# A two-layer decoder trunk on one core: r, k and v in three rounded products, sums by head in column groups, both low-rank rates together

## What is computed

```python
xx = x_prev - h
xr, xw, xk, xv, xa, xg = (h + xx * mu[j] for j in range(6))
r, k, v = xr @ w_r, xk @ w_k, xv @ w_v                       # 1024 x 1024 each
log_w = -softplus(-(dw0 + tanh(xw @ dw1) @ dw2)) - 0.5       # rank 64
a = sigmoid(aw0 + (xa @ aw1) @ aw2)                          # rank 64
g = sigmoid(xg @ gw1) @ gw2                                  # rank 128
kk = heads(k * k_k); kk = kk / max(sqrt(sum(kk * kk, -1)), 1e-12)
# state per head: S = S * w + (S @ -kk) kk*a + v k ;  y = S @ r   (scan over tokens)
y = groupnorm(y) * ln_w + ln_b + sum(r * k * r_k, -1) * v
out = (y * g) @ w_o
```

## Time and profile before

| | us |
|---|---|
| median of 3 runs | 3864.74 |
| lowest, highest | 3859.37, 3880.96 |
| the profiled execution | 3877.49 |
| its span, first to last instruction | 3875.8 |
| PE busy, matrix products | 3598.1 (93%) |
| DVE, ACT, POOL busy | 1759.1, 943.7, 525.5 |
| mean granted TensorE clock | 0.951 |

### The profile page before, as it was taken

One profiled execution on the slowest core, in us unless ns is written; L12 is line 12 of the kernel. 1 busy time (PEld: TensorE's weight loads), 2 busy tenths in 40 slices (PEclk: granted clock), 3 DMA queues, 4 the chain that ended last, 5 costly groups with the idle time before them and its releaser, 6 DMA issues.

```text
span 3875.8 us, 61931 instructions
## 1 busy us (share of the span) xinstructions
PE 3598.1 (93%) x23964; PEld 3078.7 (79%) x23964; DVE 1759.1 (45%) x3204; ACT 943.7 (24%) x1787; POOL 525.5 (14%) x220
## 2 busy tenths in 40 slices
PE   9999998998999999969999588989899899999997
PEld 6667666667999999946567477778785699999996
DVE  3545543116444444461240467655631544444444
ACT  2223324302111111111001455555520211111111
POOL 0000000001111122101000122223221121111120
PEclk9999999999999999989999789999869999999998
DMA  2222114402111111022111101000051111111101
GB/s 96 59 73 62 52 40 143 141 0 68 52 43 43 43 43 43 0 82 86 45 67 45 68 12 40 29 23 23 20 162 43 55 44 43 43 43 43 43 22 45
DMA packets 151310, 206.35 MB, mean 53 GB/s; under 512 B 42542, under 2 KB 126433, under 8 KB 150786
## 3 DMA queue, kind: packets, MB, share of 16 engines
q1 hardware_dynamic: 145122, 184.55, 14.4%
q0 software_dynamic: 6048, 19.73, 1.6%
HBM read 173.87 MB, written 50.82 MB: 58 GB/s over the span
## 4 chain that ended last, share of the span: by engine, by line
PE 64%; issue 7%; DVE 5%; PEld 4%; ACT 2%; DMA 1%; SPq 0%; POOL 0%; ACTq 0%; PEldq 0%; DVEq 0%; POOLq 0%
PE bank L429 61%; PEld bank L429 4%; PE bank L437 3%; DVE arena L2437 1%; DVE arena L2430 1%; ACT arena L2016 1%; DVE arena L2213 1%; DVE hT L2522 1%; DVE std L2210 0%; SPq L1260 0%; ACT arena L1943 0%; DVE n L2213 0%; DMA arena<-arena 0%; DVE arena L2456 0%; DVE arena L2504 0%
## 5 line engine op out<-in xcount | busy, mean ns | idle before, releaser
L429 PE MATMUL bank<-arena 128*128 128x384 f32 (+20 forms) x9432 | 1562.3, 351 | 142.2 <-ACT arena L1682 28.5
L429 PEld LDWEIGHTS bank<-arena 128*128 128x128 f32 (+11 forms) x9432 | 1124.7, 181 | 560.7 <-issue 171.2
L2225 DVE TENSOR_TENSOR hT<-hT,bank 128x384 f32<-128x384 f32 (+1 forms) x816 | 426.4, 526 | 523.5 <-PE bank L429 523.5
L429 PE MATMUL bank<-n_hi,up_hi 128*128 128x384 f32 (+1 forms) x1536 | 502.3, 327 | 27.2 <-DVE n_lo L2382 14.2
L1682 ACT COPY arena<-bank 128x512 f32<-128x512 f32 (+12 forms) x573 | 264.6, 497 | 1035.2 <-PE bank L429 755.4
L429 PE MATMUL bank<-u_hi,dn_hi 128*128 128x384 f32 (+1 forms) x1536 | 501.1, 326 | 0.0
L429 PE MATMUL bank<-u_lo,dn_hi 128*128 128x384 f32 (+1 forms) x1536 | 499.9, 325 | 0.0
L429 PE MATMUL bank<-n_hi,up_lo 128*128 128x384 f32 (+1 forms) x1536 | 499.6, 325 | 0.0
L429 PE MATMUL bank<-n_lo,up_hi 128*128 128x384 f32 (+1 forms) x1536 | 499.6, 325 | 0.0
L429 PE MATMUL bank<-u_hi,dn_lo 128*128 128x384 f32 (+1 forms) x1536 | 496.0, 323 | 0.0
L1521 POOL TENSOR_TENSOR up_lo<-arena,up_hi 128x2048 fp32r<-128x2048 f32 x32 | 151.2, 4725 | 1590.9 <-ACT up_hi L1838 1590.9
(11 more groups left out here) (181 smaller groups left out, 2903.5 us busy)
## 6 DMA issues: line engine op xcount, KB each, us to landing
arena<-in_ffn_w_up SPq DMA_DIRECT2D x32, 1024.0 KB, 5.4
arena<-in_ffn_w_down SPq DMA_DIRECT2D x32, 1024.0 KB, 7.4
arena<-past_scratch SPq DMA_DIRECT2D x32, 640.0 KB, 8.1
past_scratch<-in_cache_kv_latent SPq DMA_DIRECT2D x128, 128.0 KB, 2.4
hidden_scratch<-hT SPq DMA_DIRECT2D x1, 4288.0 KB, 13.8
past_scratch<-in_cache_k_rope SPq DMA_DIRECT2D x128, 32.0 KB, 2.1
arena<-in_rwkv_w_r SPq DMA_DIRECT2D x4, 1024.0 KB, 5.2
r_scratch<-arena POOLq DMA_DIRECT2D x8, 512.0 KB, 5.2
```

Source lines behind the costliest of these rows:

```text
L429: return pe.matmul(out, lhsT, rhs, start=first, stop=last, skip_group_check=group)
L2225: lane.do(dve.tensor_tensor(hT[:, k, at:at + w], hT[:, k, at:at + w], b[:, 0:w], ALU.add), ring.drained)
```

## The change

**Mixing stage.** r, k and v use three rounded products as the MLPs do. The differences are formed once (`DX`, by pieces), the mixed input `x_mix` exists for r, k and v only, by pieces; ACT rounds it to `x_hi`, DVE subtracts for `x_lo` (which lies where `x_mix` lay). ACT rounds each weight block to `w_hi`, POOL subtracts for `w_lo`. `x_hi` lies on `hT`, whose content is stored by then. The low-rank inputs are no longer mixed: since (h + xx·mu) @ w = h @ w + xx @ (mu·w), PE forms `nT` with the plain weights and adds `DX` with the weights times mu. dw1 and aw1 do this together, ahead of r; gw1 does it between r and k. All is written out, without loops.

```diff
+            def lora_sums(b, weights, acts, p, first, last):
+                at, w = PIECES[p]
+                for k in range(KT):
+                    ins = mm(b[:, 0:w], weights[:, k, :], acts[:, k, at:at + w], first and k == 0, last and k == KT - 1)
+                return ins
...
+            pe.wait_ge(wl_s, 32)
+            three = []
+            for p in range(3):
+                pe.wait_ge(norm_s, mark["normed1"] + p + 1)
+                three.append(ra.bank(ahead=p))
+                lora_sums(three[p], w_wa, nT, p, True, False)
+            pe.wait_ge(mu_s, 1)
+            for p in range(3):
+                pe.wait_ge(dx_s, p + 1)
+                ra.done(lora_sums(three[p], w_mu, DX, p, False, True))
+            pe.drain().then_inc(lora_used, 1)
```

```diff
             big(0, False)
-            lora_in(1, wl)
-            big(2, False)
-            lora_in(3, wl)
-            big(4, True)
-            lora_in(5, wg)
+            pe.wait_ge(wl_s, 48)
+            pe.wait_ge(mu_s, 2)
+            for p in range(3):
+                b = ra.bank()
+                lora_sums(b, w_g, nT, p, True, False)
+                ra.done(lora_sums(b, w_mu, DX, p, False, True))
+            big(1, False)
+            big(2, True)
```

```diff
+            for m in range(3):
+                mixed(m, 0)
+                mixed(m, 1)
+                split_mixed(m, 0)
+                mixed(m, 2)
+                split_mixed(m, 1)
+                split_mixed(m, 2)
+                if m == 0:
+                    dve.wait_ge(lora_used, 1)
+                    dve.wait_ge(wl_s, 48)
+                    dve.tensor_tensor(w_mu[:, :, :], w_g[:, :, :], prm[:, :, R_MU + 5:R_MU + 6].broadcast_to([P, KT, P]), ALU.mult).then_inc(mu_s, 1)
```

```diff
+            def big(m, token_major):
+                for blk in range(4):
+                    hi, lo = w_hi[blk % 2], w_lo[blk % 2]
+                    pe.wait_ge(wlo_s, 4 * m + blk + 1)
+                    for p, (at, w) in enumerate(PIECES):
+                        if blk == 0:
+                            pe.wait_ge(xlo_s, 3 * m + p + 1)
...
+                                    out = b[0:rows.stop - rows.start, u * 256:(u + 1) * 256]
                                     for k in range(KT):
-                                        ins = mm(b[0:w, u * 256:(u + 1) * 256], x[:, k, t * P:t * P + w], wb[par][:, k, :],
-                                                 k == 0, k == KT - 1)
+                                        mm(out, x_hi[:, k, rows], hi[:, k, :], k == 0, False)
+                                        mm(out, x_hi[:, k, rows], lo[:, k, :], False, False)
+                                        ins = mm(out, x_lo[:, k, rows], hi[:, k, :], False, k == KT - 1)
...
+                                cols = slice(m_ * P, (m_ + 1) * P)
+                                b = ra.bank()
+                                for k in range(KT):
+                                    mm(b[:, 0:w], hi[:, k, cols], x_hi[:, k, at:at + w], k == 0, False)
+                                    mm(b[:, 0:w], hi[:, k, cols], x_lo[:, k, at:at + w], False, False)
+                                    ins = mm(b[:, 0:w], lo[:, k, cols], x_hi[:, k, at:at + w], False, k == KT - 1)
+                                ra.done(ins)
+                        if blk == 3:
+                            through(xu_t)
+                    through(wbu_t)
+                    mark["blocks"].append(ra.filled.n)
```

```diff
+            split_weights(0)
+            for n in range(12):
+                if n + 1 < 12:
+                    split_weights(n + 1)
+                store_block(n)
```

```diff
+                pair = [ra.bank(ahead=1), ra.bank(free=True)][::-1]
+                ends = []
+                for k in range(4):
+                    for z in range(2):
+                        rows, ct = slice(z * RN, (z + 1) * RN), 4 * half + k
+                        ends.append(mm(pair[z][:, k * w:(k + 1) * w], w_lora[rows, ct * P:(ct + 1) * P], lc[rows, 0:w], True, True))
+                for ins in ends[-2:]:
+                    ra.done(ins)
...
+                for j in range(2):
+                    at = MIXTAB["head_cols"][0] + 2 - 2 * j
+                    for g in range(4):
+                        ins = mm(bank[32 * g:32 * g + 32, 0:w], mixtab[:, at:at + 32], kx[:, 4 * j + g, 0:w], j == 0, j == 1)
...
                 level_16(c, 0, ma, lambda: turn_b_k(c, P))
-                if prepare:
-                    decays(c + 1, wn, [0])
                 level_32(c, 0, ma, lambda: bonus_sums(c, P))
                 bonus_at = ra.filled.n - 1
                 v_in[par].wait(pe, nth)
                 level_64(0, ma, [when(prepare, lambda: key_sums(c + 1, wn)), lambda: first_sums(0), lambda: turn_bonus(P, bonus_at)])
-                finals(0, when(prepare, lambda: decays(c + 1, wn, [1])), when(prepare, lambda: key_scales(c + 1, wn)))
+                finals(0, when(prepare, lambda: rates(c + 1, wn, 0)), when(prepare, lambda: (rates(c + 1, wn, 1), key_scales(c + 1, wn))))
```

```diff
+                    for dst, row in ((sw, R_DW0), (rate, R_AW0)):
+                        b = ring.bank()
+                        for k in range(4):
+                            ct = 4 * half + k
+                            ins = act.activation(dst[:, ct, 0:w], b[:, k * w:(k + 1) * w], ACT.Sigmoid,
+                                                 bias=prm[:, ct, row:row + 1])
+                        lane.do(ins, ring.drained)
+                        if half == 1:
+                            signal(act.drain(), sw_b if dst is sw else rate_b)
...
                 spread_32(c, 0)
-                if prepare:
-                    decay_rates(c + 1, wn)
                 take_w_32()
...
-                    key_rates(c + 1, wn)
+                    both_rates(c + 1, wn)
                 spread_16(c, 1)
                 if prepare:
                     decays(c + 1, wn, wn == TAIL)
```

```diff
                 if finish:
                     centre(c - 1, P, Y[1 - par])
                 if prepare:
-                    sums(c + 1, wn, wn == TAIL)
...
                 new_half(0)
                 if prepare:
                     normed_keys(c + 1, wn)
+                    sums(c + 1, wn, wn == TAIL)
```

345 lines of the change are left out of this document (167 added, 178 removed).

## The result

The changed kernel takes **3766.96 us** (median of four, 3762.13 to 3772.5) where the kernel before takes 3870.38 beside it (3859.37 to 3880.96): a ratio of **0.9734, 95% interval 0.9700 to 0.9767**, 103 us less. Beside the kernels of the last experiments it has the ratio 0.9733 (0.9709 to 0.9758). The forecast was 3745 us; the range of 3705 to 3785 holds the time, the forecast's own range of 3727 to 3765 misses it by 2 us.

What follows compares the result with a forecast made beforehand. PE's products were taken to bound the mixing stage, the chain PE, ACT, PE the chunks. Stage -81, chunks -34 and preparation -5 made -120, 3745 us beside 3864.74; own range 3727 to 3765, wider range 3705 to 3785.

Steps and rivals of the forecast that it cites:

- r, k: Mixing stage: a rounded block takes 23.95 us instead of 30.0; r takes 97.8 us and k 96.7.
- v: Mixing stage: 0.120 us per product of 256 columns, 26.4 a block, 106 us where 129.6 stood.
- Rival (d): v's products pay weight load and columns one after another, 0.226 us each; kernel 3836 us; chance 0.02.
- Supply: Mixing stage: splitting the next block's weights on ACT and POOL takes 15.6 us, hidden in 23.4 with eight to spare.
- Rival (f): Supply fails: POOL late in each block, back to 30 us a block; kernel 3818 us; chance 0.02.
- Start: Mixing stage: first big product 26.0 us behind nT, 20.0 before; DVE slowdown beside POOL's subtraction, bounds 0 and 4.7, taken as none.
- Chunks: Chunk loop: -5.2 us a chunk from its path, 1 taken back for the clock; 8 x 4.2, -34.
- The level of 32 to that of 64: In a chunk, first row of 32 to second of 64: 6.65 us instead of 10.90, -4.25.
- The finals: In a chunk: less filler and halved key_scales give -1.35 us, later ACT and DVE work reduces it to -0.95.
- The clock: In a chunk: granted clock falls behind idle stretches with less filler; 1 us a chunk allowed, bounds 0 and 3.
- Rival (a): Chunks keep their time through low clock or late sums and sums_before; gain 10 instead of 34, 3769 us; chance 0.17.
- Rival (e): PE's less dense work keeps the clock low for most of a chunk; kernel slower, 3929 us; chance 0.02.

Runs made afterwards that it cites:

- start_split: Changed kernel with the first block's weight subtraction on DVE instead of POOL and the low-rank banks emptied before the second rounding; 3760.28 us, ratio 0.9689.
- gate_last: Changed kernel with the gate's low-rank products moved from between r and k to behind v; 3760.20 us, ratio 0.9683.
- stage_alone: Changed kernel with all chunk changes taken back, so only the mixing stage is the changed one; 3798.52 us, ratio 0.9814 to the kernel before.
- joined_more: As joined, with four and three fillers instead of three and two, and two more ahead of the next chunk's before_keys; 3723.82 us, ratio 0.9625.
- after_again: The changed kernel, unaltered, measured once more beside other kernels of the study; 3766.09 us, ratio 0.9733.
- chunks_alone: Changed kernel with the mixing stage of the kernel before, so only the chunk stage is the changed one; 3845.94 us, ratio 0.9928.
- rates_apart: Changed kernel with the rates formed together undone (sigmoids again ahead of take_w_32), sums by head still in column groups; 3818.01 us, ratio 0.9865.
- the other -9.5: Changed kernel with the sums by head serial again, eight products into 16 rows, rates still formed together; 3788.99 us, ratio 0.9784.
- pad_both: Changed kernel with three fillers ahead of the first half's level of 32 and two ahead of the second half's level of 16; 3739.77 us, ratio 0.9632.
- joined: Changed kernel with the edits of pad_both, gate_last and start_split in one; 3746.45 us, ratio 0.9678.
- rates_apart_pad: As rates_apart, with three fillers of 256 columns behind the sum by head of the level of 32; 3766.37 us, ratio 0.9735.

## Why the prediction was right, and where it was not

**The base.** The forecast stood beside a median of 3864.74; that of the four runs beside after is 3870.38. So 5.6 of the 22 us between 3745 and 3767 are no fault of a step. The change in time was forecast as -120 and measured as -103, with an interval of -116 to -90. Added up from the profiles (stage -77.7, preparation -4.3, seven chunks -23.9, rest -8.4, each mean of after's code less mean of before's) it is -114; the eleven that are left lie within what two profiles of before's chunks differ by (8.5) and the interval.

**r, k.** Right: 24.0 us from store to store against the 23.95 of the sum; the product of 384 columns is that of the earlier trace rows. From its first product on r took 98.6 us, 97.8 forecast, and k 97.5 with the wait ahead of v, 97.7 forecast.

**v.** Right: 26.03 from store to store, forecast 26.4; PE was busy 103.04 us for 861 records, 0.120 each, the value taken between bounds of 0.107 and 0.139. So the 384 and 304 rows less their columns did foretell the width that no row showed. Rival (d), by the rule of the Trainium skill (TensorE: Matmul & The Clock Gate, "Part 3: Packing small matmuls — row/col tiling") on weight loads that overlap only in another row group, would have had 0.226; the trace doesn't agree with it, as PEld is busy for 101.64 of the same 105.00 us in which PE is busy for 103.04.

**Supply.** Right: POOL never held PE inside a block. k to v waits about 1 us. Rival (f) is out. The gate's products took 28.7 us (1858.90 - 1830.22), 29.5 forecast.

**Start.** The 26.0 from nT on is 25.7 in the trace, with the named wait for the low-rank banks. But nT itself came 4.0 late: 34.1 us behind the store of `hT` (1705.9 - 1671.8) instead of 30.1 (1690.8 - 1660.7). This was the term with bounds 0 and 4.7 of which I took none, and it came out at its upper end; start_split shows the cause. The Trainium skill (SBUF — State Buffer, "SBUF: two separate sides") says that a DVE operation with two inputs in SBUF and a GpSimd operation that reads SBUF lock each other out for a whole instruction; the trace agrees (8.60 = 4.32 + 4.28 beside a POOL operation of 4.51). I had not drawn on it, and with the rule the upper bound would have been the value to take.

**End.** Right: 6.8 us from the end of v to the meeting, 6.5 forecast, and gate_last wins it back. Stage in all: -77.7 for -81. From nT on it took 362.9 us, 363.5 forecast; what is missing is the 4.0 ahead of nT.

**Chunks.** The sum, -4.2 each, nearly hit (seven chunks -3.4 each, from the means of the table, and more in the last and the tail: -32 in all for -34), but not by its terms. A chunk of stage_alone, whose chunks are those of before, and the same chunk of after, at a mean clock of 0.98 and 0.91, PE (first row of the level of 32, second row of 64, first wide product and level of 16 of the second half); stage_alone, begun at 2206.89:

```profile
2215.08 1.15 PE L443 MATMUL bank<-arena,hT 64*64 64x64 f32 x32 [1.03 <-ACT arena L2046]
...
2225.98 1.14 PE L443 MATMUL bank<-arena,hT 64*64 64x64 f32 x16
...
2246.69 1.14 PE L443 MATMUL bank<-arena 64*128 64x256 f32 x8 [0.51 <-DVE hT L2584]
...
2251.23 1.12 PE L443 MATMUL bank<-arena,hT 64*64 64x32 f32 x32 [1.70 <-DVE hT L2615]
```

and after, begun at 2206.76:

```profile
2214.95 1.97 PE L443 MATMUL bank<-arena,hT 64*64 64x64 f32 x32 [3.02 <-ACT arena L2045]
...
2223.84 1.11 PE L443 MATMUL bank<-arena,hT 64*64 64x64 f32 x16 [0.33 <-ACT arena L1710]
...
2244.24 1.13 PE L443 MATMUL bank<-arena 64*128 64x256 f32 x8 [1.09 <-DVE hT L2580]
...
2249.58 1.12 PE L443 MATMUL bank<-arena,hT 64*64 64x32 f32 x32 [2.50 <-DVE hT L2611]
```

Three steps can be read off.

- *The level of 32 to that of 64.* Forecast 6.65, here 8.89. The path was right, the clock was not: at full clock it is 6.49 (joined_more), 4.4 less than the 10.90 of the earlier trace rows, where -4.25 was forecast. The prediction had seen that PE would wait 2.8 ahead of the level (it waits 3.02) and had put the price of the clock behind all such waits at 1 us a chunk; this one place costs 1.5 (chunk 5) to 2.4.
- *The finals.* They were to bring 0.95 us and cost 0.5. After leads by 2.0 us at the second row of 64 (19.09 against 17.08 from the chunk's start), by 2.3 us where the second half's wide products begin (2246.69 - 2206.89 = 39.80 against 37.48), and by 1.5 at the level of 16, which waits 2.50 for DVE's X4 instead of 1.70. "DVE's next masks begin 0.4 later" was measured from the end of SA and held nearly (PE waits 1.09 for them instead of 0.51), but the chain behind was costed at DVE's free speed. Of after:

```profile
2235.35 2.04 DVE L2514 TENSOR_TENSOR arena<-arena 128x512 f32<-128x512 f32 x1
...
2242.90 3.79 DVE L2580 TENSOR_TENSOR hT<-bank,arena 128x512 f32<-128x512 f32 x6
2246.80 2.03 DVE L2552 SCALAR_TENSOR_TENSOR arena<-arena 128x1024 f32<-128x1024 f32 x1
...
2234.49 2.35 POOL L1640 TENSOR_TENSOR arena<-arena 128x1024 f32<-128x1024 f32 x1
...
2243.06 2.37 POOL L1631 TENSOR_TENSOR arena<-arena 128x1024 f32<-128x1024 f32 x1 [6.22 <-DVE arena L2535]
2245.39 2.36 POOL L1612 TENSOR_TENSOR arena<-arena 128x1024 f32<-128x1024 f32 x1
```

  L2514 and L2552 take 1.14 and 1.23 in stage_alone, 1.7 us less, with 0.6 us of POOL beside the first and none beside the second; the change moved POOL's order (`sums_before`, L1631, now stands right ahead of L1612). Even the 1.14 isn't the free speed. Where POOL is idle the same operation takes 0.69, in after too:

```profile
2200.51 0.69 DVE L2514 TENSOR_TENSOR arena<-arena 128x512 f32<-128x512 f32 x1
```

  So it lost 1.35 us where 1.49 of it and of POOL's operation overlapped, and L2552 lost 0.80 where 0.95 did. The masks L2580, one of whose inputs is a bank, take 3.79 in both, although in after POOL ran beside nearly all of them and in stage_alone for 0.1 us. The step that failed is this one: PE waits 0.6 us more for the masks and 0.8 more for X4, 1.4 together, which is about the difference between the 0.95 forecast as gain and the 0.5 lost.
- *The clock.* At the chunk's end this pair differs by 0.46 us only (74.70 against 74.24, clock 0.98 against 0.91). The gain of after lies in the other chunks: the profiles of before and stage_alone have three chunks of 79 to 84 us among the seven, those of after and after_again none but the first over 75.2 (after's chunks inside chunks_alone and gate_last reach 78.6). At full clock on the new side (joined_more) the chunk takes 70.01, 4.7 less than 74.70 and close to the 5.2 that the path terms gave. One sign of being wrong did come: the first chunk of after has a mean clock of 0.80, below the 0.85 named, with 81.00 us where at most 78 were forecast; but it is 0.84 and 84.20 us in before, and after's other chunks have 0.91 to 0.93.

So the level's term was right but for the clock, the finals' term had the wrong sign, and the total was near by luck: the clock took more than the 1 us allowed, and took it from the kernel before as well. Rival (a), the chunks keep their time for just these two reasons, was half true; I gave it 10 us of gain, and the chunks have 24 (chunks_alone less its preparation) to 32 (the profiles). Rival (e), a gain turned round by the clock, didn't come in this kernel, but rates_apart is its picture in small: shorter work, 19.5 us slower.

**Preparation.** -4.3 for -5.

## What to carry to other kernels

Where PE waits anyway, work that is taken out ahead of the wait wins nothing, and here it cost the clock: compare the granted clock of the windows behind such a place before a term is booked as gain, and try a filler of the length that was taken out. Judge a part of a change with the waits around it filled, since one part alone gave +19.5 us here, the other -9.5, and both together -32. And look at what runs on GpSimd beside each VectorE operation with both inputs in SBUF that stands on the path.

## What the hardware did that was not expected

- The granted clock can stay at 0.50 for 18.5 us in which PE is busy all the time, and come back soon behind the same waits one chunk earlier (both in rates_apart). The same chunk of the same instructions took 69.30 us at a mean of 0.98 in one program and 79.68 in another, at 0.82 (pad_both, joined).
- Fillers are worth much more than they cost: three of 0.70 us a chunk brought 52 us in rates_apart_pad, five a chunk 27 in pad_both, and nine some 30 in joined_more (42 less the 12.6 of its stage).
- With both inputs in SBUF, a VectorE operation lost nearly all the time in which a GpSimd operation that reads SBUF ran beside it: 4.28 us beside one of 4.51, 1.35 and 0.80 where 1.49 and 0.95 overlapped. With one input from a bank (L2580) it lost nothing.
